# A two-layer attention and mLSTM network on one core: attention's fold, sums, results and gates kept by channel

## What is computed

```python
def even_mixer(h_lat, h_ctx, w_in, ...):          # h: layer norm of x, scaled and shifted
    q, ga, k, v, u, gb = jnp.split(h @ w_in, EVEN_SPLITS, axis=-1)   # 768, 768, 256, 256, 256, 256
    q, k = rms_norm(q), rms_norm(k)               # 12 query heads, 4 key heads of 64; rope on latent ones
    # latent queries attend to all 2304 keys, context queries to the 256 of the context
    a = softmax(q @ k.T / 8) @ v
    f = real(fft2(rms_norm(u))) @ w_fmix          # over tokens and 64 channels of a group
    y = concatenate([a * silu(ga), f * silu(gb)]) @ w_out
# around it: x = layer_norm(ALPHA * x + g * y) * gain + bias
```

## Time and profile before

| | |
|---|---|
| median of three runs | 3728.18 us (3726.63 to 3730.16) |
| profiled execution: its span (no other time is given for it) | 3728.3 us |
| busy share of PE, DVE, POOL, ACT | 92%, 62%, 49%, 36% |
| DRAM traffic | 339.75 MB read, 137.72 MB written |

### The profile page before, as it was taken

How to read it: one execution, slowest core, us unless ns; L and a number is a source line. 1 busy time by engine, 2 the same in 40 slices (tenths; PEclk the granted TensorE clock), 3 DMA queues, 4 the chain that set the end, 5 groups by cost and what they waited for, 6 DMA issues and landing times. The chain is left out here.

```text
span 3728.3 us, 51376 instructions
## 1 busy us (share of the span) xinstructions
PE 3437.4 (92%) x16884; PEld 2591.3 (70%) x16884; DVE 2295.2 (62%) x3492; ACT 1333.6 (36%) x2240; POOL 1839.1 (49%) x1294
## 2 busy tenths in 40 slices
PE   6999996799999999999859979989999998999798
PEld 4787884456666666666558869877778786887586
DVE  4666642766666666666436654366575644777576
ACT  2432333444444444444320123333443422664200
POOL 1133313667777777777623333423586612444364
PEclk7999997799999999999979989999999999999899
DMA  5234535511111111111064535555545446677563
GB/s 189 99 106 132 149 100 187 179 27 37 37 37 34 34 35 34 34 35 34 19 214 163 191 134 179 204 184 160 170 130 172 145 149 197 215 221 240 198 214 135
DMA packets 357715, 480.18 MB, mean 129 GB/s; under 512 B 83308, under 2 KB 209276, under 8 KB 357392
## 3 DMA queue, kind: packets, MB, share of 16 engines
q1 hardware_dynamic: 291744, 342.18, 29.9%
q10 hardware_dynamic: 54256, 97.73, 8.7%
q0 software_dynamic: 11520, 37.77, 2.6%
HBM read 339.75 MB, written 137.72 MB: 128 GB/s over the span
## 5 line engine op out<-in xcount | busy, mean ns | idle before, releaser
L2259 DVE TENSOR_REDUCE al_mx<-al_sx 128x1 f32<-128x512 f32 (+1 forms) x960 | 562.2, 631 | 268.8 <-PE al_sx L2336 255.3
L2199 ACT ACTIVATE al_e<-al_st 128x1024 f32<-128x1024 f32 x432 | 442.7, 1025 | 580.3 <-PE al_st L2349 570.4
L2229 POOL TENSOR_TENSOR al_acc_p<-al_acc_p,al_e 128x1024 f32<-128x1024 f32 x192 | 456.6, 2378 | 19.7
L235 PE MATMUL pb_acc<-p_whi,pb_r_hi 128*128 128x512 f32 x952 | 380.5, 400 | 37.9 <-DVE pb_r_lo L1606 28.5
L2358 PE MATMUL al_acc<-al_e,vres 128*64 128x512 f32 x1728 | 402.6, 601 | 0.0
L237 PE MATMUL pb_acc<-p_whi,pb_r_lo 128*128 128x512 f32 x952 | 376.8, 396 | 0.0
L236 PE MATMUL pb_acc<-p_wlo,pb_r_hi 128*128 128x512 f32 x952 | 376.6, 396 | 0.0
L1606 DVE TENSOR_TENSOR pb_r_lo<-pb_stg,pb_r_hi 128x512 fp32r<-128x512 f32 x238 | 248.7, 1048 | 169.1 <-ACT pb_r_hi L1504 164.8
L2348 PE MATMUL al_st<-al_qa,kres 128*128 128x512 f32 x864 | 345.0, 399 | 3.7 <-DMA al_qb<-al_negm 3.3
L2349 PE MATMUL al_st<-al_qb,kres 128*128 128x512 f32 x864 | 340.5, 394 | 0.0
L2336 PE MATMUL al_sx<-kres,al_qx 128*128 128x512 f32 (+1 forms) x960 | 298.6, 394 | 14.5 <-DMA al_qx<-s_q 12.2
(11 more groups left out here) (320 smaller groups left out, 7285.1 us busy)
## 6 DMA issues: line engine op xcount, KB each, us to landing
pb_stg<-s_hsum ACTq DMA_DIRECT2D x238, 256.0 KB, 2.7
s_proj<-pj_stage SPq DMA_DIRECT2D x90, 256.0 KB, 2.1
s_proj<-pb_out SPq DMA_DIRECT2D x72, 256.0 KB, 3.1
p_wst<-in_w1s ACTq DMA_DIRECT2D x18, 1024.0 KB, 6.9
ml_k<-s_proj SPq DMA_DIRECT2D x36, 512.0 KB, 4.3
ml_v<-s_proj SPq DMA_DIRECT2D x36, 512.0 KB, 8.8
mo_in<-s_proj SPq DMA_DIRECT2D x34, 512.0 KB, 6.0
hm_w<-in_ada_w SPq DMA_DIRECT2D x16, 1024.0 KB, 8.9
```

The costliest lines, as they stand in the source:

```text
L235: nc.tensor.matmul(out, s_hi, m_hi, start=start, stop=False)
L2199: nc.scalar.activation(e[:, pair(p, j), :, :], st[(NP * p + j) % 2][:, :, 0:W], ACT.Exp).then_inc(e_done, 1)
L2229: nc.gpsimd.tensor_tensor(acc_p[:], acc_p[:], e[:, pair(p, j)], ALU.add).then_inc(add_p, 1)
L2259: V.tensor_reduce(mx[:, x:x + 1], slots[x % NSX][:, 0:spans[x % NS][1]], AX.X, ALU.max).then_inc(sx_max, 1)
```

## The change

Results stay by channel (channels on partitions, tokens along the free axis) from attention, the gates and the Fourier part up to the first output product, so this product needs no transposes. The gates' two chunks of the projection are computed with the weights as the stationary operand and pairs of token tiles as the moving one, as `projections` already can (`turned_q`). In attention the fold table and a 128 by 64 block of ones are the stationary operands and 512 queries move; the sums come out once for each of 64 partitions, and the reciprocal is taken of all of them. The context's attention does the same with 64 columns of ones beside the values. Fourier results stay in SBUF (`four`). To make room, `QueryHeads` has two row buffers instead of three and keeps its squares in the product's place, and some of Fourier's buffers lie in rows that have been used.

```diff
 class QueryHeads:
+        self.px = self.x[:, 2 * QW:4 * QW].rearrange("p (c h d) -> p c h d", c=2, d=HD)
+        self.sq = self.px[:, 0]
     def load(self, sp, t):
-        if t >= 3:
-            sp.wait_ge(self.sq_done, t - 2)
-            sp.wait_ge(self.px_done, t - 2)
-            sp.wait_ge(self.table_done, t - 2)
+        if t >= 2:
+            sp.wait_ge(self.sq_done, t - 1)
+            sp.wait_ge(self.px_done, t - 1)
+            sp.wait_ge(self.table_done, t - 1)
     def squares(self, act, t):
-            act.wait_ge(self.ss_done, t)
+            act.wait_ge(self.turn_done, 2 * t)
     def products(self, dve, t):
         dve.wait_ge(self.table_done, t + 1)
+        dve.wait_ge(self.ss_done, t + 1)
 def projections(nc, m, a, s, keep, layer, cols=None, dec=None):
-    K, RING, NST, NACC, PIECES, NX = len(steps), 3 if L0 else 4, 3, 3, 2, 3
+    K, RING, NST, NACC, PIECES, NX = len(steps), 4, 3, 3, 2, 3
-    turned_q = [not L0 and C1_Q <= c * CH < C1_Q + D for c, _ in steps]
+    turned_q = [c >= GATED if L0 else C1_Q <= c * CH < C1_Q + D for c, _ in steps]
-                    sp.dma_start(s["qt"][row:row + 2 * P, token:token + 2 * P].rearrange("(j p) n -> p j n", p=P),
+                    sp.dma_start(s["gt"][row:row + 2 * P, token:token + 2 * P].rearrange("(j p) n -> p j n", p=P),
 class ContextAttention:
-        self.nc.vector.memset(self.v1[:, :, :, HD:HD + 1], 1.0).then_inc(self.fixed, 1)
+        self.nc.vector.memset(self.v1[:, :, :, HD:], 1.0).then_inc(self.fixed, 1)
     def values(self, pe, n):
-        for i in range(CT):
-            for t in range(CT):
-                x = self.nc.tensor.matmul(self.res[:, i, 0:HD + 1], self.e[:, n % 2, t, i * P:(i + 1) * P], self.v1[:, t, n // QPK, :], start=(t == 0), stop=(t == CT - 1))
+        for t in range(CT):
+            x = self.nc.tensor.matmul(self.res[:, 0:self.W], self.v1[:, t, n // QPK, :], self.e[:, n % 2, t, :], start=(t == 0), stop=(t == CT - 1))
     def norm(self, dve, n):
-        self.nc.vector.reciprocal(self.rden[:, n % 2, :], self.res[:, :, HD]).then_inc(self.rden_done, 1)
+        self.nc.vector.reciprocal(self.rden[:, n % 2, :], self.res[HD:P, 0:self.W]).then_inc(self.rden_done, 1)
         dve.wait_ge(self.rden_done, n + 1)
-        self.nc.vector.tensor_tensor(self.o[:, n], self.res[:, :, 0:HD], self.rden[:, n % 2, :].unsqueeze(2).broadcast_to([P, CT, HD]), ALU.mult).then_inc(self.o_done, 1)
+        self.nc.vector.tensor_tensor(self.o[:, n], self.res[0:HD, 0:self.W], self.rden[:, n % 2, :], ALU.mult).then_inc(self.o_done, 1)
 def attention(nc, m, a, s, keep, kres, vres, tag, q0, nq, nb, nk):
-                sp.dma_start(s["attn"][rows, bass.ds(h * HD, HD)].rearrange("(t p) d -> p t d", p=P), o[:, p % NO]).then_inc(stored[p % 2], 16)
+                sp.dma_start(s["attn"][bass.ds(h * HD, HD), cols], o[:, p % NO, :]).then_inc(stored[p % 2], 16)
             def norm(n, p, v):
-                V.reciprocal(rden[:], fo[:, 0:nq * (HD + 1)].rearrange("p (s d) -> p s d", s=nq)[:, :, HD]).then_inc(rden_done, 1)
+                V.reciprocal(rden[:], fo[HD:P, 0:W]).then_inc(rden_done, 1)
...
-                V.tensor_tensor(o[:, p % NO], fo[:, 0:nq * (HD + 1)].rearrange("p (s d) -> p s d", s=nq)[:, :, 0:HD],
-                                rden[:].unsqueeze(2).broadcast_to([P, nq, HD]), ALU.mult).then_inc(o_done, 1)
+                V.tensor_tensor(o[:, p % NO, :], fo[0:HD, 0:W], rden[:], ALU.mult).then_inc(o_done, 1)
             def folded(n, p):
-                for i in range(nq):
-                    at, cols = i * (HD + 1), slice(i * P, (i + 1) * P)
-                    mm(fo[:, at:at + HD], ot[:, p % 2, cols], fold[:, 0:HD], start=True, stop=True)
-                    y = mm(fo[:, at + HD:at + HD + 1], asum[:, p % 2, cols], ones[:], start=True, stop=True)
-                y.then_inc(fold_mm, 1)
+                mm(fo[0:HD, 0:W], fold[:, 0:HD], ot[:, p % 2, :], start=True, stop=True)
+                mm(fo[HD:P, 0:W], ones[:], asum[:, p % 2, :], start=True, stop=True).then_inc(fold_mm, 1)
 def fourier(nc, m, a, s, keep, out_weights, four):
-            for n, (y, flip) in enumerate(outs):
...
-                sp.dma_start(rows.rearrange("(m r) c -> r m c", r=R)[R - r if flip else r], o[:, n % NO, :]).then_inc(stored[n % NO], 16)
-                if n % 2 and 2 + n // 2 < KD:
-                    out_weights.load(sp, 2 + n // 2)
-            for i in range(NO):
-                sp.wait_ge(stored[i], 16 * (len(outs) // NO))
+            for k in range(2, KD):
+                out_weights.load(sp, k)
...
-                V.tensor_copy(o[:, n % NO, :], po[n % 2][:, 0:FW]).then_inc(o_out, 1)
+                V.tensor_copy(tokens.rearrange("p h (m r) -> p h m r", r=R)[:, :, :, R - r if flip else r],
+                              po[n % 2][:, 0:FW].rearrange("p (h m) -> p h m", h=2)).then_inc(o_out, 1)
...
-                        mm = nc.tensor.matmul(po[n % 2][:, h * P:(h + 1) * P], src[:, y % 2, 2 * h + c, :], g[:, 2 if flip and c else c, h, :], start=(c == 0), stop=(c == 1))
+                        mm = nc.tensor.matmul(po[n % 2][:, h * P:(h + 1) * P], g[:, 2 if flip and c else c, h, :], src[y % 2][:, 2 * h + c, :], start=(c == 0), stop=(c == 1))
 def mixer_out(nc, m, a, s, keep, layer, out, out_weights, following=None, four=None):
-                sp.wait_ge(y_done[p], v)
+                if not L0:
+                    sp.wait_ge(y_done[p], v)
+                elif not (isinstance(n, int) and n < 2):
+                    sp.wait_ge(lo_done, n - 1)
-                    sp.dma_start(ins[:, p, 0, 0:QW], s["attn"][rows, :]).then_inc(in_ld[p], 16)
-                    sp.dma_start(ins[:, p, 0, QW:D], s["four"][rows, :]).then_inc(in_ld[p], 16)
-                    sp.dma_start(ins[:, p, 1, :], s["proj0"][rows, C_GATE:W0_COLS]).then_inc(in_ld[p], 16)
+                    sp.dma_start(ins[:, p, 0, 0:QW].rearrange("p (k n) -> p k n", n=P), s["attn"][:, rows].rearrange("(k p) n -> p k n", p=P)).then_inc(in_ld[p], 16)
+                    sp.dma_start(ins[:, p, 1, :].rearrange("p (k n) -> p k n", n=P), s["gt"][:, rows].rearrange("(k p) n -> p k n", p=P)).then_inc(in_ld[p], 16)
             def gated(n, p, v):
+                if L0:
+                    dve.wait_ge(in_ld[p], 32 * v + 32)
+                    tokens = bass.ds(n * P, P)
+                    nc.vector.tensor_tensor(columns(p)[:, 0:KA, :], ins[:, p, 0, 0:QW].rearrange("p (k n) -> p k n", n=P),
+                                            ins[:, p, 1, 0:QW].rearrange("p (k n) -> p k n", n=P), ALU.mult)
+                    nc.vector.tensor_tensor(columns(p)[:, KA:KD, :], four[:, :, tokens],
+                                            ins[:, p, 1, QW:D].rearrange("p (k n) -> p k n", n=P), ALU.mult).then_inc(y_done[p], 1)
+                    return
             def turned(n, p, v):
+                if L0:
+                    return
```

More of the change, by code:

```diff
@@ L2572, in _ @@
             V.tensor_scalar(z[:, 1:H:2, 2, :], z[:, 1:H:2, 1, :], -1.0, None, ALU.mult).then_inc(odd_done, 1)
-            for n in range(len(outs)):
+            for n, (y, flip) in enumerate(outs):
+                j, r, _ = sums[y]
+                R = jobs[j][1]
+                tokens = four[:, :, 0:CTX] if j == 0 else four[:, :, CTX:T]
                 dve.wait_ge(o_mm, n + 1)
-                if n >= NO:
-                    dve.wait_ge(stored[n % NO], 16 * (n // NO))
-                V.tensor_copy(o[:, n % NO, :], po[n % 2][:, 0:FW]).then_inc(o_out, 1)
+                V.tensor_copy(tokens.rearrange("p h (m r) -> p h m r", r=R)[:, :, :, R - r if flip else r],
+                              po[n % 2][:, 0:FW].rearrange("p (h m) -> p h m", h=2)).then_inc(o_out, 1)
         @block.scalar
@@ L2652, in _, with mixer_out @@
                 mixed(n)
-def mixer_out(nc, m, a, s, keep, layer, out, out_weights, following=None):
+def mixer_out(nc, m, a, s, keep, layer, out, out_weights, following=None, four=None):
     L0 = layer == 0
@@ L2673, in mixer_out @@
     stats, mv, rstd, half = m.sb(tag + "stats", [P, 2, 6]), m.sb(tag + "mv", [P, 2]), m.sb(tag + "rstd", [P, 1]), m.sb(tag + "half", [P, 1])
-    tp, acc = [m.ps(tag + f"tp{i}", (P, 2, 512)) for i in range(2)], [m.ps(tag + f"acc{i}", (P, 2, 512)) for i in range(2)]
+    tp, acc = [] if L0 else [m.ps(tag + f"tp{i}", (P, 2, 512)) for i in range(2)], [m.ps(tag + f"acc{i}", (P, 2, 512)) for i in range(2)]
+    KA = QW // P
+    columns = lambda p: y[:, p, :].rearrange("p (k n) -> p k n", n=P) if L0 else tp[p][:].rearrange("p a (k n) -> p (a k) n", n=P)
     const = m.sem(tag + "const")
@@ L2732, in high_part @@
             def high_part(n, p, v):
-                act.wait_ge(tr_done, n + 1)
+                if L0:
+                    act.wait_ge(y_done[p], v + 1)
+                else:
+                    act.wait_ge(tr_done, n + 1)
                 if not (isinstance(n, int) and n < 2):
                     act.wait_ge(mm_done, n - 1)
```

(8 more changed lines are left out.)

79 lines of the change are left out of this document (38 added, 41 removed).

## The result

The changed kernel takes 3757.5 us in the median of four runs (3751.2 to 3758.8) against 3729.2 (3726.6 to 3740.8) for the kernel before beside it: a ratio of 1.0068, 95% interval 1.0054 to 1.0082. By the medians it is slower by 28 us, by the ratio by 25 (20 to 31), where 10 were forecast. The median lies 1.5 us above the range; the ratio, taken of the 3728.2 us that the forecast started from, gives 3753.5, just inside it. Its profiled execution took 3757.7 us over a span of 3755.8, which is 27.5 more than the earlier trace rows.

The account below looks back on a forecast made before the run. PE was taken to bound attention and the first output product, with DVE and POOL nearly full in the heads. 3728.3 + 9.3 + 25.0 - 9.2 + 3.7 - 14.7 - 4.0, less 0.1, gave 3738 us; range 3712 to 3756.

Parts of the forecast that it names:

- Step 1: Projection, gates' product turned: 36 steps go from 5.44 to 5.70 us, no added wait, +9.3 us.
- Step 2: Reciprocal on DVE in attention and context attention: 8.0 ns an element, 4.25 us for 512, 2.2 us for 256.
- Rival B: Reciprocal costs some 6.5 ns an element; whole 3730 us, no measurable change; chance 0.15.
- the page's price: Reciprocal by the Trainium skill's page: 8.3 ns an element, 4.4 and 2.3 us, whole sum 3741 us.
- Step 3: Context attention in the heads stage, 12 heads: 21.9 us for slower DVE, 3 for PE's low clock, +25 us.
- Rival D: Heads stage: PE at half clock and DVE wait in turn, another 1.2 us in 12 tiles, 3752 us; chance 0.08.
- Step 4: Attention, 48 blocks: PE gains 0.69 us, waits 0.41 for a maximum; 46 blocks -9.2 us, the last +3.7.
- POOL's ring: Attention: POOL's combined sum, DVE's first add, then x8's maximum, needed by PE's x11; slack 0.35 us, 0.25 after handoff.
- Rival C: Attention: reciprocal above 4.3 us lengthens the block one for one; at 5.2 us the whole is 3781 us; chance 0.06.
- Step 6: First mixer's output product: period 11.80 to 10.88 us, -14.7 us for 16 tiles; its start -4.0 us.
- PE idle in the mixer behind DMA: First mixer: a sign named in advance that the forecast was wrong; its loads were taken as covered.
- Step 5: Fourier: products swap operands, 18 stores and reading back go; the stage ends with POOL's weight split, so 0 us.

Follow-up runs that it names:

- three such edits: Gate multiplies ahead of the normalisation, h prepared three steps ahead, two buffers for acc_d, together on the changed kernel: 3718.4 us against 3730.5 for the kernel before, ratio 0.9965.

## Why the prediction missed

The sign was right. The forecast difference was 18 us too low against the medians; in the profiled executions it was 17 too low, 13 without the start that isn't the change's. That the ratio falls inside the range owes as much to the range's width as to the steps, of which two failed:

**Step 1, the gates' product, failed.** It had 9.3 us and measured 22.1. "RING grows to 4 and it is still prepared two steps ahead, so I add no wait" is the sentence that was wrong: a pair wants both its tiles at its first step, DVE's queue has QueryHeads' work in it, and PE waited for `h_lo` and behind it for `hq_lo`, 10 us. The starts came 0.120 us apart, not 0.119, so the step grew by 0.32 us, not 0.26 (2.2 us over 36). QueryHeads' two buffers at 0 were nearly right (1.2).

**Step 2, the reciprocal, was over-sized:** 6.25 ns an element, not 8.0; 3.36 and 1.76 us for 4.25 and 2.2. The rows of before gave 6.0 between four elements and one, and 8.0 from the other instruction. Two lengths of the same operation gave the better slope. The Trainium skill's repeat count of eight (VectorE: DVE Perf Modes, "First, the fixed hardware budget"), which had seemed to support 8, isn't what these rows show: 6.25 ns is six cycles at the page's 0.96 GHz. Rival B had nearly the price (6.5), yet not the time (3730), because the other steps had missed. The 3741 given for the page's price is also too low by the forecast's own walk, in which another 0.17 us lengthen each of 46 blocks: 3747.

**Step 3, the heads, was right in its sum by luck: two errors cancelled.** 21.9 for DVE and 3 for the clock were forecast; the split of the ten windows, scaled to the stage's 25, gives some 15 and 10. DVE's part was over-sized because the reciprocal was, and because DVE did not fill the stage before: POOL was as busy. Rival D's mechanism, DVE's work and a low clock in PE together, was at work, with a smaller DVE part than mine. And the stage's own spread (129.7 and 138.6 without the change) is a third of the 25.

**Step 4, attention, was right in mechanism, with one ring too many.** PE's gain was 0.57 us where POOL doesn't bind, for 0.69, and 0.23 in every second block of the loops, for the 0.25 that the walk left to POOL's ring. The steady blocks gained 0.27 in the mean (12.3 over 46) for 0.2. Of the two rings named, POOL's was the true one: the second buffer for acc_d removed PE's waits but for 0.4 us. The wait at x3 for the maximum behind the reciprocal was not there, because the reciprocal was 0.9 us shorter; with two in a row both it and the longer one at x2 came where the walk put them. (Rival C's "above 4.3 us" is x2's point; by the walk blocks grow from 3.84 on, at x3.) The last block was over-sized: forecast at +3.7, it cost 1.9. From its fold to the last `al_o` are 5.41 us instead of 3.80, and the product is 0.3 longer: the reciprocal was 0.9 shorter than taken, and the fold gave back 1.0 us more than the 0.6 taken.

**Step 6, the output product, failed.** It priced the period from PE alone: 10.88. DVE's second multiply was given 0.06 us; beside POOL's addition it takes 2.6, DVE waits another 0.72 for a `rstd` that, by the rows, its own low part holds up, and the period is 11.38. That is 8 of the 9 us by which the stage missed. "PE idle in the mixer behind DMA" was watched for, DVE wasn't, though its instructions and POOL's stood in the trace of before, where the one multiply started 0.16 us ahead of POOL's addition, which took 3.31 us beside it:

```profile
2095.88 1.22 DVE L2829 TENSOR_TENSOR mo_y<-mo_in 128x1024 f32<-128x1024 f32 x1
2096.04 3.31 POOL L2761 TENSOR_TENSOR mo_fin<-mo_fin,mo_beta 128x1024 f32<-128x1024 f32 x1 [2.26 <-DVE mo_fin L2819]
```

**Step 5 and the start of step 6** together gave 7.3 us for 4.0. From POOL's last split to the mixer's first product are 10.1 us instead of 15.7, so 5.6 lie there, for the 4.0 forecast; the other 1.6 lie ahead of the split's end, in Fourier, where 0 was forecast. What shortened Fourier wasn't tried.

## What to carry to other kernels

Turning an operand to relieve the engine that bounds the work also changes which instruction of the other engines starts first, and when a pair of tiles must be ready: look for the next ring in each stage, and give it a buffer or an earlier place, before judging the change. Here three such edits, worth 33 us in their stages, turned +28 us into -12. And before a reduction's result is moved to the free axis, price the operation on it by its length: a reciprocal is cheap over four elements and long over 512, free where DVE has room, and dear where DVE is the bound.

## What the runs showed of the hardware

- A reciprocal on DVE of fp32 results of PE takes 6.25 ns for each element of a partition and 0.16 us beside (3358 ns for 512, 1759 for 256).
- A DVE multiply with both inputs in SBUF that starts during a POOL addition waits for its end (2.62 us for 0.42, 3.15 for 0.95), and POOL's waits for DVE's in turn (3.04 and 3.31 for 2.40). A POOL operation on one element took 1.07 us beside a DVE operation with two SBUF inputs, and 0.18 beside one that took one of them from PE's result.
- Two fp32 matmuls of 64 columns each start 0.01 us apart in the two halves of PE's columns, the second pair 0.48 later.
- With a wait of 2.3 us of PE in every block, most blocks have a granted clock of 0.94 and take 26.8 us; those at 1.00 take 25.2.
